# Two merges of branches that work in the PSUM bank, and input tables of a scan that start without waiting for stored output tables

## The reference

```
# second block
gate_rwkv, gate_att = jnp.split(jax.nn.sigmoid(p_gate), N_BRANCH, axis=-1)
merged = gate_rwkv * (y_rwkv @ w_branch_rwkv[l]) + gate_att * (y_att @ w_branch_attn[l])
x = x + merged @ w_out[l]

# third block
merged = jax.nn.sigmoid(g_sb) * y_sb + jax.nn.sigmoid(g_ssm) * y_ssm      # y_sb, y_ssm: 512 -> 1024
return merged @ w_out
```

## Time and profile before

| | us |
|---|---|
| median of three executions | 3437.56 |
| the profiled execution | 3438.88 |
| its span on the core | 3437.1 |
| PE busy | 3354.5 (98%) |
| POOL busy | 1868.0 (54%) |
| DVE busy | 1632.8 (48%) |
| ACT busy | 756.1 (22%) |

### The profile page before, as it was taken

The page is one execution under the profiler, slowest core; times in us unless marked ns, Lnnn a source line. Parts: engine busy times, 40 slices in busy tenths (PEclk is TensorE's granted clock), DMA queues, the critical chain, the costliest instruction groups (busy, mean ns, idle before and its releaser), DMA issues.

```text
span 3437.1 us, 46356 instructions
## 1 busy us (share of the span) xinstructions
PE 3354.5 (98%) x19426; PEld 2660.4 (77%) x19426; DVE 1632.8 (48%) x2754; ACT 756.1 (22%) x1595; POOL 1868.0 (54%) x1459
## 2 busy tenths in 40 slices
PE   8999999999999999999999988999999999999998
PEld 7768788986788887888788787788877776778886
DVE  6554443558444444342532855562436657541223
ACT  2241011356411012000202531200012135120001
POOL 7526566631265676766664004666666511756663
PEclk9999999999999999999999999999999999999999
DMA  5203334220124343342232003332335534423221
GB/s 174 81 25 110 129 104 147 90 79 26 38 98 135 107 138 110 99 135 92 93 98 98 3 3 115 113 98 87 97 98 191 168 108 139 146 68 100 91 98 37
DMA packets 253680, 340.76 MB, mean 99 GB/s; under 512 B 9760, under 2 KB 186144, under 8 KB 250912
## 3 DMA queue, kind: packets, MB, share of 16 engines
q1 hardware_dynamic: 230960, 301.51, 26.9%
q10 hardware_dynamic: 22512, 36.28, 3.1%
HBM read 308.15 MB, written 25.43 MB: 97 GB/s over the span
## 4 chain that ended last, share of the span: by engine, by line
PE 88%; DVE 7%; POOL 2%; ACT 2%; DMA 1%; issue 1%; ACTq 0%; DVEq 0%; SPq 0%; POOLq 0%
PE bank L125 87%; PE bank L128 2%; POOL wlo L148 1%; DVE scr L148 1%; POOL whi L155 0%; DVE st L163 0%; POOL raw L148 0%; DVE p L155 0%; ACT L143 0%; DMA raw<-in_w_mlp_in 0%; DVE x L148 0%; DVE BK L148 0%; DVE al L158 0%; DVE macc L158 0%; DMA raw<-in_a_w_in 0%
## 5 line engine op out<-in xcount | busy, mean ns | idle before, releaser
L155 POOL TENSOR_SCALAR whi<-raw 128x1024 fp32r<-128x1024 f32 x481 | 549.3, 1161 | 1498.4 <-PE bank L125 814.1
L148 POOL TENSOR_TENSOR wlo<-raw,whi 128x512 fp32r<-128x512 f32 x962 | 1299.3, 1382 | 20.1
L125 PE MATMUL bank<-ah,whi 128*128 128x512 f32 x2408 | 958.0, 398 | 8.1 <-ACT ah L143 4.5
L125 PE MATMUL bank<-ah,wlo 128*128 128x512 f32 x2408 | 951.4, 395 | 0.0
L125 PE MATMUL bank<-al,whi 128*128 128x512 f32 x2408 | 940.0, 395 | 1.0 <-DVE al L158 1.0
L125 PEld LDWEIGHTS bank<-ah,whi 128*128 128x128 f32 x2408 | 451.6, 188 | 127.6 <-ACT ah L143 8.2
L125 PEld LDWEIGHTS bank<-al,whi 128*128 128x128 f32 x2408 | 451.2, 188 | 112.4 <-DVE al L158 1.8
L125 PEld LDWEIGHTS bank<-ah,wlo 128*128 128x128 f32 x2408 | 451.5, 187 | 110.4 <-issue 0.2
L125 PE MATMUL bank<-hh,whi 128*128 128x512 f32 x1040 | 412.4, 397 | 0.0
L125 PE MATMUL bank<-hl,whi 128*128 128x512 f32 x1040 | 410.8, 395 | 0.0
L125 PE MATMUL bank<-hh,wlo 128*128 128x512 f32 x1040 | 410.7, 395 | 0.0
(11 more groups left out here) (451 smaller groups left out, 3982.3 us busy)
## 6 DMA issues: line engine op xcount, KB each, us to landing
raw<-in_w_in SPq DMA_DIRECT2D x34, 1024.0 KB, 5.3
raw<-in_w_mlp_in SPq DMA_DIRECT2D x32, 1024.0 KB, 5.5
raw<-in_w_mlp_out SPq DMA_DIRECT2D x32, 1024.0 KB, 7.4
raw<-in_w_ada SPq DMA_DIRECT2D x24, 1024.0 KB, 5.3
raw<-in_ffn_w_gate SPq DMA_DIRECT2D x22, 1024.0 KB, 5.3
raw<-in_ffn_w_up SPq DMA_DIRECT2D x22, 1024.0 KB, 5.3
raw<-in_ffn_w_down SPq DMA_DIRECT2D x22, 1024.0 KB, 5.0
raw<-in_w_ffn_in SPq DMA_DIRECT2D x22, 1024.0 KB, 5.1
```

Source lines behind the costliest of these rows:

```text
L125: return self.eng.matmul(out, lhsT, rhs, start=start, stop=stop, skip_group_check=True)
L148: return IDLE if self.eng is None else self.eng.tensor_tensor(out, a, b, op)
L155: return self.eng.tensor_scalar(out, a, s1, s2, op0, op1)
```

## The change

Two things are changed.

In the second branch of both merges, the product with the gate and the sum with the other branch are written back into the PSUM bank, not into an SBUF tile of `scr`, and ACT rounds from the bank. The low part of a tile is taken behind the sum of the next tile, and reads the bank. The bank is given up by the low part (before: by the product). The gate's tile is given up by the product, as before.

In the tables, DVE's wait for the store of the round before moves from the head of the input tables to the head of the output tables.

```diff
@@ merge_act
-                a.f(self.ah[:, m, :], self.scr.of(name, m)[:, :], ACT.Copy).then_inc(*self.C.up(name, "hi", m))
+                a.f(self.ah[:, m, :], self.ps.of((name, half, br), n)[:, :], ACT.Copy).then_inc(
+                    *self.C.up(name, "hi", m))
@@ merge_dve
+        def low(m):
+            key = ((name, m // 4, 1 - T["first"]), m % 4)
+            d.wait_ge(*self.C.at(name, "hi", m))
+            d.tt(self.al[:, m, :], self.ps.of(*key)[:, :], self.ah[:, m, :].bitcast(F), SUB).then_inc(
+                *self.ps.give(D, *key))
+            D.mark(name, m)
...
-                g = self.sq.of(name, half, br, n)
-                if second:
-                    s, free = self.scr.take(name, m)
-                    d.wait_ge(*free)
+                g, bank = self.sq.of(name, half, br, n), self.ps.of(*key)
                 d.wait_ge(*self.P.at(*key))
                 d.wait_ge(*self.gate_in[i % 2].at(name, half, br, n))
                 i += 1
-                dst = s[:, :] if second else T["gr"][half][:, n, :]
-                d.tt(dst, self.ps.of(*key)[:, :], g[:, :], MUL).then_inc(*self.ps.give(D, *key))
-                self.sq.also(D, name, half, br, n)
-                if second:
-                    d.wait_ge(*D.now())
-                    d.tt(s[:, :], s[:, :], T["gr"][half][:, n, :], ADD).then_inc(*D.up(name, "value", m))
-                    d.wait_ge(*self.C.at(name, "hi", m))
-                    d.tt(self.al[:, m, :], s[:, :], self.ah[:, m, :].bitcast(F), SUB).then_inc(
-                        *self.scr.give(D, name, m))
+                if not second:
+                    d.tt(T["gr"][half][:, n, :], bank[:, :], g[:, :], MUL).then_inc(*self.ps.give(D, *key))
+                    self.sq.also(D, name, half, br, n)
+                    continue
+                d.tt(bank[:, :], bank[:, :], g[:, :], MUL).then_inc(*self.sq.give(D, name, half, br, n))
+                d.wait_ge(*D.now())
+                d.tt(bank[:, :], bank[:, :], T["gr"][half][:, n, :], ADD).then_inc(*D.up(name, "value", m))
+                if m:
+                    low(m - 1)
+        low(7)
@@ tables_dve
         if j:
             d.wait_ge(*self.P.at("tables", j - 1, "KS", 1))
-            d.wait_ge(*self.tab_out["WC"].at(j - 1))
         p3 = lambda n: self.ssm_par(n).rearrange("p (q c) -> p q c", q=16)
         self.outer_dve(d, "XB", [t["XB0"], t["XB1"]], [m["b0"], m["b1"]], 8, j, True)
+        if j:
+            d.wait_ge(*self.tab_out["WC"].at(j - 1))
         self.outer_dve(d, "WC", [t["WC0"], t["WC1"]], [p3("c_re"), p3("c_im")], 9, j, False)
```

## The result

The changed kernel took 3444.47 us (median, 3442.4 to 3448.56) against 3437.62 us of the kernel before (3436.76 to 3442.38), 16 executions of each. The ratio is 1.0019, 95% interval 1.0012 to 1.0027: 6.9 us, or 0.2%, slower. The interval leaves out 1, so the change does make the kernel slower, by just less than the 0.2% under which the prediction would have called it no change. The forecast was 3444.9 us, with a range of 3439.5 to 3450. The profiled execution took 3444.73 us with a span of 3442.9 us, 5.8 us more than before, where the sum gave 6.0.

What follows compares the result with a forecast made beforehand. PE, busy 98% of the span, was taken as the bound. Waits 2.7 + 4.0, tails 0.5 + 1.0, clock 1.5, tables -2.0 - 1.7 gave +6.0 us on the profiled 3438.88: 3444.9 us, range 3439.5 to 3450.

Steps and rivals of the forecast that it cites:

- The held bank: First merge (second block): PE's fourth group waits for the low part of the third group's second tile, +2.7 us.
- The second merge: Third block's merge: the same wait ahead of the fourth group, with 3.7 us for the gate's transfer, +4.0 us.
- Rival (b): Gates land late, 4.8 us in both merges: +2.1 and +1.1 us, 3448.1 us; chance 0.15.
- The clock: PE's clock behind the merges' waits: first merge's loss left at 1.5 us, second gains a fall, +1.5 us.
- Rival (a): Slow clock stretch runs out by itself within the merges' waits: 1.9 us less, 3443.0 us; chance 0.20.
- Behind the fourth groups: Output projections wait for banks given up later by low parts: +0.5 us first merge, +1.0 us second.
- The tables: Round 1's XB starts earlier, so PE's 2.04 us wait and the clock's fall go: -2.0 and -1.7 us.
- Rival (e): Round 1's XB late from POOL contention, or the moved wait stops WC; tables give nothing, 3448.6 us; chance 0.05.
- (c): Merges' gate transfers do not bind, landing with the second tile's work: 0.6 and 1.6 us less, 3442.7 us; chance 0.08.
- (d): Fourth group gets other banks and does not wait for low parts; merges cost nothing, 3435.2 us; chance 0.05.

Runs made afterwards that it cites:

- e3: Tables as changed, low part a tile later, but product and sum in scratch tiles, bank given up by the product; 3431.15 us, 0.9982 of the kernel before.
- e5: Kernel after with low parts taken in pairs behind the sum of every second tile; 3437.71 us, 0.9996 of the kernel before.
- e1: Kernel after with the tables' wait put back, so the merges' change alone; 3449.08 us, 1.0032 of the kernel before.
- e4: Kernel after with 18 products that nobody reads on PE ahead of each fourth group; 3441.79 us, 1.0011 of the kernel before.
- e2: Kernel before with only the tables' wait moved; 3433.70 us, 0.9989 of the kernel before.
- e8: Kernel after with scratch tiles for the merges' third group, banks kept for the fourth; 3432.24 us, 0.9981 of the kernel before.
- e10: e8 without the ten unread products of the first projection, the second's four kept; 3430.10 us, 0.9975 of the kernel before.

## Why the prediction was right, point by point

**The held bank: right, by its steps.** The chain was predicted as 6.66 us in the first merge (1.53 + 2.7 + 2.43) and took 6.61; the start moved by 2.6 us against the 2.7 of the sum. e3 and e5 show the cause from both sides: give the bank up at the product, and the wait falls to 0.31; take the low part from behind the third tile's gate, and it falls to 2.32. The price of a write to the bank, taken as 0.75 from a range of 0.69 to 0.79, is 0.70. The rows of a bank operand read beside an SBUF operand were the right neighbours.

**The second merge: a term mis-sized.** I took 3.7 us for its gate from the transfer of before; it took 2.7. The start moved by 2.9 us, not 4.0. The step that failed is the 3.7 us for this gate. The landings vary: DVE waited 0.91 us for this gate in the kernel after and 1.62 in e1, and PE's wait in e1 was longer by as much (5.19 us for 4.49). In e4 DVE waited for two gates, 0.49 and 1.43 us, and PE's group began 5.75 us after the third. What sets the landing stays open. Rival (b) put it down to the weight load beside it, but the mean DMA share over the transfer was 0.66 before, where it took 3.7 us, and 0.91 after, where it took 2.7.

**The clock: right in the second merge, too small in the first.** +1.5 was forecast for the second, +1.4 came. The first was left at 1.5 in all and became 2.3 (11.66 - 9.37). There the low stretch lasted 6.8 us, twice that of before, and began 2.6 us after PE had stopped. This is the second term that was mis-sized.

**Rival (a) fell on this.** A stretch of 3.4 us that runs out by itself would have had 1.9 of them in the first merge's wait and left a loss of 0.75. The stretch began in the wait and did not end there: 1.9 us of it passed idle, and then 4.87 us of work ran at 0.50. The second merge of the kernel after shows no stretch that began early enough to judge by. That of e1 does: the clock was down for the last 2.93 us of the wait and for 3.77 us of work behind it. Windows of e1 (columns as before):

```profile
2973.50:2976.43 2.93, 0.01 (x1) 0.50 0.20 69
2976.43:2980.20 3.77, 3.77 (x9) 0.50 0.46 150
```

The Trainium skill (TensorE: Matmul & The Clock Gate, Part 1) has the low clock as the default, which activity lifts; by that rule the stretch does not run out in the wait. The 4.87 and 3.77 us of work at 0.50 behind an idle stretch agree. That PE would then pay the time of my sum did not follow: it paid 2.3 us in the first merge, not 1.5. I left that term as it was before, and no row that I showed had a stretch longer than 3.6 us. The trace of the kernel before does have longer ones, of 6.8 us near 779 and near 2015 us, so a bound from it would have been wider. Why the stretch was 6.8 us long here and 3.4 in the second merge stays open.

**Behind the fourth groups: right in kind, small in size.** +0.5 and +1.0 were forecast, +0.3 and +0.5 came, both ahead of the products that nobody reads, where the text put them. PE goes on in the first at T + 2.17 (2159.76 - 2157.59) and not T + 2.43, in the second at T + 4.10 (2985.36 - 2981.26) and not T + 4.57. The steps were reckoned with 0.75 us each; the measured ones lie 0.74 apart where the next instruction reads what the last wrote (2139.32 to 2140.06) and 0.60 where it doesn't (2140.06 to 2140.66).

**The tables: right.** -3.7 was forecast, -3.9 came in the profile, 3.8 and 4.5 by the ratios of e2 and e1. XB took 9.18 us beside POOL and was still 1.94 us ahead of PE. Rival (e) needed more than 11.3.

**The other rivals.** (b) wanted late gates: they landed in 2.8 and 2.7 us. (c) wanted gates that do not bind: DVE waited 0.98 and 0.91 us for them. (d) wanted other banks: the wait for `al` stands ahead of both fourth groups.

**What was not in the sum.** +1.4 us come from a fall of the clock at 2587.8 that no step of the change explains. Without it the span would have grown by 4.4. With the 0.7 us that the first merge's clock had beyond the sum, it made up for what the second merge's term had too much (1.1 us) and the tails (0.7). The base of the forecast helped too: the 6.0 us were added to one execution that lay 1.3 us above its median. Added to the median they give 3443.6 us, and the medians grew by 6.9. That the total met the forecast to 0.4 us in the median is in part luck.

**The sums in the bank.** DVE's sums went from a median of 0.93 to 0.70 us. The Trainium skill (SBUF — State Buffer, Who interferes with whom) states that a DVE instruction with at most one SBUF input, outside its 2-port modes, doesn't contend with GpSimd; the low parts agree on both sides, with 0.68 us from a bank and up to 1.78 from `scr` in one and the same kernel (e8). It is a true gain, and it was spent where nobody waits for DVE's busy time but for a bank.

## What to carry to other kernels

Before work is moved to a buffer of a ring, ask which instruction gives the buffer up afterwards and what stands ahead of that one in its engine's program; here a transfer for another tile did, and 0.2 us saved per sum cost PE 2.6 us in one merge and 2.9 in the other, before the clock. Work in place where the next user of the buffer is far off, and copy out where it is waited for: the edit in the bank for the fourth group alone, with scratch tiles and a late low part for the third, the tables as changed, and the 14 products that nobody reads removed, gave the lowest time of the study (3430.03 us, 0.26% under the kernel before). Most of this came from giving the third group's banks up at the product and from the tables: scratch tiles in both groups (e3) are at 0.18% under, and the intervals do not tell the two apart. And price a wait of the matrix engine with the clock behind it, 1.4 to 2.6 us here.

## What the runs showed of the hardware that was not expected

The granted clock is not the same from one execution to the next. With the same instructions ahead, it was at 0.50 near 780 us for 0 (e2), 3.4 (e5), 6.8 (before), 10.2 (after) and 13.7 us (e1).

The idle time just ahead does not tell whether the clock falls. After 1.91, 2.04, 2.32 (e5, twice) and 4.5 us it fell, after 1.60 and 1.49 (e4) it didn't; but behind small products it also fell after 0.78 us (at 2587.8 in the kernel after; the same 0.78 us in the kernel before brought no fall) and 0.79 us (e10). And 4.55 us idle brought a stretch of 6.8 us at 0.50 while 4.49 us brought one of 3.4.

A subtraction on DVE of 512 columns with both operands in SBUF took 1.78 us beside POOL, 2.6 times the 0.68 us of the same subtraction with one operand in a bank.
